# Experts in falling order of their token counts, with 112 to 64 slots by place, in a transformer block kernel on one Trainium2 core

## What is computed

```
def moe_ffn(h, router, w_gu, w_d):
    logits = (h @ router).astype(jnp.float32)
    top_logits, top_idx = lax.top_k(logits, TOP_K)          # TOP_K = 2
    weights = jax.nn.softmax(top_logits, axis=-1)
    combine = jnp.sum(jax.nn.one_hot(top_idx, N_EXPERTS) * weights[..., None], axis=-2)
    for e in range(N_EXPERTS):                              # N_EXPERTS = 8
        out = out + combine[..., e:e + 1] * swiglu(h, w_gu[e], w_d[e])
```

## Time and profile before

| | us |
|---|---|
| median of three runs | 2742.36 |
| span of the profiled execution | 2739.1 |
| expert stage, first gather to end of the last down product | 1580.7 to 2723.0 |
| TensorE busy | 2562.2 (94%) |
| VectorE busy | 654.7 (24%) |
| ScalarE busy | 482.4 (18%) |

### The profile page before, as it was taken

How to read it: one execution, slowest core, us unless ns; L and a number is a source line. 1 busy time by engine, 2 the same in 40 slices (tenths; PEclk the granted TensorE clock), 3 DMA queues, 4 the chain that set the end, 5 groups by cost and what they waited for, 6 DMA issues and landing times.

```text
span 2739.1 us, 61321 instructions
## 1 busy us (share of the span) xinstructions
PE 2562.2 (94%) x28155; PEld 1852.2 (68%) x28156; DVE 654.7 (24%) x1091; ACT 482.4 (18%) x809; POOL 45.5 (2%) x146
## 2 busy tenths in 40 slices
PE   6999878999999998879798899999999999999998
PEld 3564723444478777867786686878778786969593
DVE  1033433000001367737677210000000000000001
ACT  3123013000001265432432310000000000000000
POOL 0000002100000000000000000000000000000000
PEclk9998989999999999989997899999999999999999
DMA  7245004322234600054002278888888888889793
GB/s 250 82 164 184 1 31 154 117 77 77 77 123 159 210 31 3 4 179 169 3 5 73 108 254 324 295 319 306 312 308 317 302 317 302 322 301 336 284 349 138
DMA packets 182197, 504.49 MB, mean 184 GB/s; under 512 B 9586, under 2 KB 73412, under 8 KB 175796
## 3 DMA queue, kind: packets, MB, share of 16 engines
q1 hardware_dynamic: 180148, 494.27, 50.9%
q0 software_dynamic: 1792, 6.19, 0.7%
HBM read 499.38 MB, written 1.05 MB: 183 GB/s over the span
## 4 chain that ended last, share of the span: by engine, by line
PE 55%; DVE 4%; issue 1%; ACT 1%; DMA 0%; POOL 0%; DVEq 0%; ACTq 0%; POOLq 0%
PE banks L1077 25%; PE banks L1094 14%; PE banks L855 7%; PE banks L623 3%; PE banks L1051 1%; PE banks L992 1%; PE banks L1062 1%; PE banks L803 1%; DVE ring_arena L1809 1%; DVE rstd L1915 0%; PE banks L816 0%; DMA ring_arena<-in_rw_a 0%; DVE ring_arena L1814 0%; PE banks L578 0%; DVE rstd L1783 0%
## 5 line engine op out<-in xcount | busy, mean ns | idle before, releaser
L1077 PEld LDWEIGHTS banks<-ring_arena 128*64 128x64 f32 x14336 | 687.1, 137 | 19.1 <-issue 18.2
L1077 PE MATMUL banks<-ring_arena 128*64 128x112 f32 x14336 | 694.0, 259 | 0.0
L1094 PE MATMUL banks<-ring_arena 128*112 128x512 f32 x896 | 385.8, 592 | 0.0
L623 PE MATMUL banks<-ring_arena 128*128 128x256 f32 (+1 forms) x1024 | 314.9, 467 | 15.4 <-DVE ring_arena L1615 9.3
L760 PE MATMUL banks<-ring_arena 128*128 128x512 f32 x704 | 305.4, 597 | 6.4 <-ACT ring_arena L1145 6.1
L1094 PEld LDWEIGHTS banks<-ring_arena 128*112 128x112 f32 x896 | 158.0, 177 | 221.9 <-issue 221.9
L623 PEld LDWEIGHTS banks<-ring_arena 128*128 128x128 f32 x1024 | 195.5, 192 | 134.2 <-issue 102.0
L1998 DVE TENSOR_TENSOR ring_arena<-ring_arena,banks 128x448 f32<-128x448 f32 x32 | 19.9, 621 | 1033.1 <-PE banks L1077 1033.1
L760 PEld LDWEIGHTS banks<-ring_arena 128*128 128x128 f32 x704 | 134.7, 192 | 176.3 <-issue 175.2
L855 PE MATMUL banks<-ring_arena 64*64 64x128 f32 (+1 forms) x6144 | 202.9, 256 | 38.4 <-DVE ring_arena L1814 19.0
L855 PEld LDWEIGHTS banks<-ring_arena 64*64 64x64 f32 x6144 | 190.5, 135 | 45.0 <-issue 32.1
(11 more groups left out here) (304 smaller groups left out, 1831.7 us busy)
## 6 DMA issues: line engine op xcount, KB each, us to landing
ring_arena<-in_moe_w_gu SPq DMA_DIRECT2D x256, 896.0 KB, 5.5
ring_arena<-in_moe_w_d SPq DMA_DIRECT2D x112, 1024.0 KB, 7.0
ring_arena<-in_mod_w SPq DMA_DIRECT2D x48, 1024.0 KB, 6.8
ring_arena<-in_ff_w_gu SPq DMA_DIRECT2D x22, 1024.0 KB, 5.1
ring_arena<-in_ff_w_d SPq DMA_DIRECT2D x22, 1024.0 KB, 4.9
ring_arena<-in_rw_w_rkv SPq DMA_DIRECT2D x20, 1024.0 KB, 5.4
ring_arena<-in_gla_w_in SPq DMA_DIRECT2D x12, 1024.0 KB, 5.6
ring_arena<-in_gla_w_out SPq DMA_DIRECT2D x4, 1024.0 KB, 6.4
```

Of the source, the lines that this page charges most:

```text
L623: ins = T.matmul(b[:, 0:width], w[:, k, j * P:j * P + P], src[:, k, :], start=(k == 0), stop=(k == KT - 1))
L1077: ins = T.matmul(bank[CH * h:CH * h + CH, (c % 4) * CAP:(c % 4) * CAP + CAP], w[:, kk, c * P + CH * h:c * P + CH * h + CH], XG[:, 2 * kp + ...
L1094: ins = T.matmul(ps[6 + h][0:CAP, :], HX[:, 2 * u + k, :], w[:, k, 512 * h:512 * h + 512], start=(u == 0 and k == 0), stop=(u == WD_UNITS ...
```

## The change

Eight slot counts by place, CAPS, take the place of the one CAP. Expert 0 stays first; experts 1 to 7 follow in falling order of their counts, which VectorE sorts (each against each, then sums with a one-hot table). The places are written out on TensorE, ScalarE and VectorE with their slot counts, in place of a loop; SP loads expert 0, waits for `route` and then reads the number of each further expert from a table. TensorE no longer waits for `route`. The masks of expert 0 are made before the sort. Second parts keep CAP slots, and MORE_ITEMS is worked out anew. On ScalarE the copies of the last down product stand before the loop for second parts instead of behind it. GpSimd writes the row of slot counts instead of the table of expert numbers. The storage of the banks keeps its stride of 112. The changed lines, cut to their core:

```diff
-MORE_ITEMS = (2 * SEG - 1) // CAP
+CAPS = (112, 112, 112, 88, 72, 72, 64, 64)
+
+
+def most_overflow():
+
+    most = 0
+    for parts in itertools.product(range(PARTS), repeat=NE):
+        counts, floor = [], 0
+        for e in range(NE - 1, 0, -1):
+            floor = max(floor, CAPS[e] + CAP * (parts[e] - 1) + 1 if parts[e] else 0)
+            counts.append(floor)
+        counts.append(CAPS[0] + CAP * (parts[0] - 1) + 1 if parts[0] else 0)
+        if max(counts) <= SEG and sum(counts) <= 2 * SEG:
+            most = max(most, sum(parts))
+    return most
+
+
+MORE_ITEMS = most_overflow()
+assert all(c + CAP * (PARTS - 1) >= SEG for c in CAPS)
@@ -422,8 +445,10 @@
...
-            with sp.Fori(0, NE) as e:
-                expert(e, e)
+            expert(0, 0)
+            sp.wait_ge(S["route"], 1)
+            with sp.Fori(1, NE) as r:
+                expert(sp.value_load(EXPERT[0:1, bass.ds(r, 1)], min_val=0, max_val=NE - 1), r)
@@ -534,9 +559,9 @@
...
-            pool.wait_ge(S["o_in"], HP)
-            pool.wait_ge(S["b_mm"], HP)
-            g.iota(EXPERT, pattern=[[0, PARTS - 1], [1, NE]], base=0, channel_multiplier=0).then_inc(S["consts"], 1)
+            for e in range(NE):
+                ins = g.memset(CAP_ROW[:, e:e + 1], float(CAPS[e]))
+            ins.then_inc(S["consts"], 1)
@@ -1037,9 +1062,8 @@
...
-            pe.wait_ge(S["route"], 1)
-
-            def scatter(n, q):
+
+            def scatter(n, q, cap):
...
-                T.matmul(ps[4 + h][:, :], PWT[0:CAP, t * P:t * P + P], YS[0:CAP, 512 * h:512 * h + 512],
+                T.matmul(ps[4 + h][:, :], PWT[0:cap, t * P:t * P + P], YS[0:cap, 512 * h:512 * h + 512],
...
-            def item(n, first):
+            def item(n, first, cap=CAP, cap_before=CAP):
@@ -1059,8 +1083,8 @@
...
-                            ins = T.matmul(ps[4 + q][:, (k % 4) * CAP:(k % 4) * CAP + CAP], HTM[:, t, k * P:k * P + P],
-                                           PG[:, t, :], start=(t == 0), stop=(t == 1))
+                            ins = T.matmul(ps[4 + q][:, (k % 4) * CAP:(k % 4) * CAP + cap], HTM[:, t, k * P:k * P + P],
+                                           PG[:, t, 0:cap], start=(t == 0), stop=(t == 1))
@@ -1074,16 +1098,16 @@
...
-                                    ins = T.matmul(bank[CH * h:CH * h + CH, (c % 4) * CAP:(c % 4) * CAP + CAP],
-                                                   w[:, kk, c * P + CH * h:c * P + CH * h + CH], XG[:, 2 * kp + kk, :],
+                                    ins = T.matmul(bank[CH * h:CH * h + CH, (c % 4) * CAP:(c % 4) * CAP + cap],
+                                                   w[:, kk, c * P + CH * h:c * P + CH * h + CH], XG[:, 2 * kp + kk, 0:cap],
...
                     if first:
-                        scatter(n, g)
+                        scatter(n, g, cap_before)
...
-                            ins = T.matmul(ps[6 + h][0:CAP, :], HX[:, 2 * u + k, :], w[:, k, 512 * h:512 * h + 512],
+                            ins = T.matmul(ps[6 + h][0:cap, :], HX[:, 2 * u + k, 0:cap], w[:, k, 512 * h:512 * h + 512],
...
-            with pe.Fori(0, NE) as e:
-                item(e, True)
+            for n in range(NE):
+                item(n, True, CAPS[n], CAPS[max(n - 1, 0)])
             for q in range(4):
-                scatter(NE, q)
+                scatter(NE, q, CAPS[NE - 1])
@@ -1409,27 +1433,34 @@
...
-            def down_out(n):
+            def down_out(n, cap):
                 act.wait_ge(S["wd_used"], WD_RING + WD_UNITS * n)
                 for h in range(2):
-                    C.copy(YS[0:CAP, 512 * h:512 * h + 512], ps[6 + h][0:CAP, :]).then_inc(S["yd_out"], 1)
-
-            def item(n):
-                down_out(n)
+                    C.copy(YS[0:cap, 512 * h:512 * h + 512], ps[6 + h][0:cap, :]).then_inc(S["yd_out"], 1)
...
+            def slots(bank, tiles, cap):
+                return bank[:, 0:tiles * CAP].rearrange("p (a b) -> p a b", a=tiles)[:, :, 0:cap]
+
+            def item(n, cap):
                 for q in range(2):
                     act.wait_ge(S["xg"], 2 * n + q + 1)
...
-                    C.activation(SX[:, 0:4, :], ps[0][:, 0:4 * CAP].rearrange("p (a b) -> p a b", a=4), ACT.Silu).then_inc(S["sil"], 1)
-                    C.activation(SX[:, 4:7, :], ps[1][:, 0:3 * CAP].rearrange("p (a b) -> p a b", a=3), ACT.Silu).then_inc(S["sil"], 1)
+                    C.activation(SX[:, 0:4, 0:cap], slots(ps[0], 4, cap), ACT.Silu).then_inc(S["sil"], 1)
+                    C.activation(SX[:, 4:7, 0:cap], slots(ps[1], 3, cap), ACT.Silu).then_inc(S["sil"], 1)
...
-            with act.Fori(0, NE) as e:
-                item(e)
-            items = second_items(act, lambda x, n: item(n))
-            down_out(items)
+                C.copy(PWT[0:cap, :], ps[4][0:cap, 0:SEG]).then_inc(S["pwt_out"], 1)
+            for n in range(NE):
+                down_out(n, CAPS[max(n - 1, 0)])
+                item(n, CAPS[n])
+            down_out(NE, CAPS[NE - 1])
+
+            def more(x, n):
+                item(n, CAP)
+                down_out(n + 1, CAP)
+            items = second_items(act, more)
@@ -1949,16 +1980,50 @@
...
-            for q in range(PARTS):
-                link(Vv.tensor_tensor(CMB[:, :, NE * q:NE * q + NE], EXL[:, :, :], MX[:, :].unsqueeze(2).to_broadcast([P, 2, NE]), ALU.mult))
+            link(Vv.tensor_tensor(CMB_EXPERT[:, :, :], EXL[:, :, :], MX[:, :].unsqueeze(2).to_broadcast([P, 2, NE]), ALU.mult))
             dve.wait_ge(S["pos"], 1)
 
...
-            for q in range(PARTS):
-                link(Vv.tensor_scalar(RK[:, :, NE * q:NE * q + NE], RK0[:, :, :], -1.0 - float(CAP * q), None, ALU.add))
+            link(Vv.tensor_scalar(RK[:, :, 0:1], RK0[:, :, 0:1], -1.0, None, ALU.add))
+            link(Vv.tensor_copy(COUNTS, ps[5][:, 2 * NE:3 * NE]))
+
+            def slots_of(pos, wt, cap):
+                for t in range(2):
+                    Vv.tensor_scalar(PG[:, t, 0:cap], SLOTS[:, 0:cap], pos[t], None, ALU.is_equal).then_inc(S["pg"], 1)
+                    Vv.tensor_scalar(PW[:, t, 0:cap], SLOTS[:, 0:cap], pos[t], wt[t], ALU.is_equal, ALU.mult).then_inc(S["pg"], 1)
+            slots_of([RK[:, t, 0:1] for t in range(2)], [CMB_EXPERT[:, t, 0:1] for t in range(2)], CAPS[0])
+
...
+
+            def sorted_by_rank(dst, v):
+                link(Vv.tensor_tensor(HOT_TMP, HOT, v, ALU.mult))
+                link(Vv.reduce_sum(dst, HOT_TMP, axis=AX.X))
+            link(Vv.tensor_copy(SORT_KEY, COUNTS))
+            link(Vv.memset(SORT_KEY[:, 0:1], 2.0 * SEG))
+            mine = SORT_KEY.unsqueeze(2).to_broadcast([P, NE, NE])
+            other = SORT_KEY.unsqueeze(1).to_broadcast([P, NE, NE])
+            link(Vv.tensor_tensor(SORT_GT, other, mine, ALU.is_gt))
+            link(Vv.tensor_tensor(SORT_EQ, other, mine, ALU.is_equal))
+            link(Vv.tensor_tensor(SORT_EQ, SORT_EQ, TRI[:, :, :], ALU.mult))
+            link(Vv.tensor_tensor(SORT_GT, SORT_GT, SORT_EQ, ALU.add))
+            link(Vv.reduce_sum(RANK, SORT_GT, axis=AX.X))
+            link(Vv.tensor_tensor(HOT, RANK.unsqueeze(1).to_broadcast([P, NE, NE]), by_rank, ALU.is_equal))
+            sorted_by_rank(ORDER, by_expert)
+            sorted_by_rank(EXCESS, COUNTS.unsqueeze(1).to_broadcast([P, NE, NE]))
+            for t in range(2):
+                sorted_by_rank(RK_SORTED[:, t, :], RK0[:, t, :].unsqueeze(1).to_broadcast([P, NE, NE]))
+                sorted_by_rank(CMB[:, t, 0:NE], CMB_EXPERT[:, t, :].unsqueeze(1).to_broadcast([P, NE, NE]))
+            link(Vv.tensor_scalar(RK[:, :, 0:NE], RK_SORTED[:, :, :], -1.0, None, ALU.add))
+            link(Vv.tensor_tensor(EXCESS, EXCESS, CAP_ROW, ALU.subtract))
+            for t in range(2):
...
             for q in range(PARTS - 1):
-                link(Vv.tensor_scalar(OVER[:, NE * q:NE * q + NE], ps[5][:, 2 * NE:3 * NE], CAP * (q + 1) + 0.5, None, ALU.is_gt))
+                cols = slice(NE * q + NE, NE * q + 2 * NE)
+                link(Vv.tensor_scalar(RK[:, :, cols], RK_SORTED[:, :, :], -1.0 - float(CAP * q), None, ALU.add))
+                link(Vv.tensor_copy(CMB[:, :, cols], CMB[:, :, 0:NE]))
+                link(Vv.tensor_scalar(OVER[:, NE * q:NE * q + NE], EXCESS, CAP * q + 0.5, None, ALU.is_gt))
+                link(Vv.tensor_copy(EXPERT[:, NE * q:NE * q + NE], ORDER))
             link(Vv.memset(BELOW, 1.0))
@@ -1980,30 +2045,34 @@
...
-            with dve.Fori(0, NE) as e:
-                item(e, e, True)
-            items = second_items(dve, lambda x, n: item(x + NE, n, False))
+            for n in range(NE):
+                if n:
+                    gathered(n)
+                    slots_of([RK[:, t, n:n + 1] for t in range(2)], [CMB[:, t, n:n + 1] for t in range(2)], CAPS[n])
+                hidden(n, True, CAPS[n])
+
```

(3 more changed lines are left out.)

36 lines of the change are left out of this document (19 added, 17 removed).

## The result

The changed kernel takes 2692.0 us, the kernel before 2741.1 us beside it on the same chips: ratio 0.9822, 95% interval 0.9809 to 0.9835. It is 49 us faster. The prediction was 139 us faster, 2603.7 us, with a range of 2593 to 2632. The direction held; 88 us of the gain are missing, and the result lies outside the range.

A forecast was written before the change was run, and what follows sets the result against it. TensorE was taken as the bound until loads take over. Start −3.7, places −17.9, −59.8 and −60.2, end +2.9 made −138.7 us; applied to the median of 2742.4 this gave 2603.7 us, eight-in-ten range 2593 to 2632.

The forecast's parts named there:

- What a narrower product costs: Gate/up records on TensorE: 38.3 ns at 88 slots, 31.6 at 72, 29.9 at 64, instead of 48.26.
- When the loads take over: Expert stage: loads at 410 GB/s set a period of 112.4 us at 64 slots; TensorE sets 112.7 at 72, 124.6 at 88.
- The term for the five narrow places: Places 4 to 8: −17.9 us for 88 slots, −59.8 for two of 72, −60.2 for two of 64.
- waits for loads in the last two places: Two places of 64 slots: 112.4 us each by their loads, against 109.6 by TensorE alone.
- a clock that falls in waits: TensorE's granted clock falling in waits for loads of about 0.6 us between units, at two experts' ends; given no case.
- the first rival: Expert weights load at 360 instead of 410 GB/s: four narrow experts about 119.7 us each, 29 us more, 2633; chance 0.15.
- The columns' pace: Gate/up records on TensorE take (2c/2.4 + 3.2)/2 ns for c slots: 38.3 at 88, 31.6 at 72, 28.3 at 64.
- The start: First expert's masks come before the sort, so TensorE's first gather starts 3.7 us earlier.
- The end: ScalarE's second-parts loop now stands behind the last down product's copies, before the first square: 2.9 us later.
- No place spilled: Spill rival: a count over its place's slots in the expert stage adds a ninth pass, 147 us, 2751; chance 0.02.
- The floor rival: Narrow gate records have a higher floor: 2668 us at 40 ns, 2741.6 at 48.26; chance 0.09.
- Its sign for that rival: Records above 32 ns in the last four experts with no wait for loads would prove the forecast record floor wrong.

The follow-up runs named there:

- light_loads: Changed kernel with each gate unit loading only one eighth of its columns, same matmuls, output wrong: 2620.5 us, ratio 0.9565 to the kernel before.
- spread: Changed kernel with each down product cut into three lumps between gate/up groups and ScalarE's last copies behind the second-parts loop: ratio 0.9806 to the kernel before.
- slots112: Changed kernel with 112 slots in every place, all else kept: ratio 0.9995 to the kernel before.
- woven1: As woven, but with down matmuls behind every gate unit instead of every second: 2645.8 us, ratio 0.9672 to the kernel before.
- woven: Changed kernel with down matmuls behind every second gate unit of groups 2 to 4, ScalarE's last copies behind the second-parts loop: 2623.0 us, ratio 0.9596.
- wide1_tail: Changed kernel, narrow places' first column tile per unit one 128-column matmul, not two of 64; ScalarE's last copies behind the second-parts loop: 2675.5 us, ratio 0.9779.

## Why the prediction was wrong

**The step that failed** is the gate time of the narrow places in "What a narrower product costs", and the account of bounds in "When the loads take over". It named three bounds of a record (columns, weight load, loads of weights) and left out the fourth, the supply of instructions. The term for the five narrow places was −137.9 us and measured 662.9 − 5 × 142.54 = −49.8. The 88 us between them come in parts. The gaps are 68.5 us. The records themselves took 70.7 + 124.1 + 119.2 = 314.0 us where 68.6 + 113.3 + 107.2 = 289.1 were forecast, 24.9 more: 34.6 ns a record at 72 slots (124.1 us / 3584) against 31.6 in an uncut group of light_loads. And the 5.6 us that the forecast gave to waits for loads in the last two places (112.4 against 109.6 each) did not come: 68.5 + 24.9 − 5.6 = 87.8.

The 24.9 us have two sources. Each run costs about 0.17 us more than its records alone (4.22 us for 128 at 72 slots, where 128 × 31.6 ns are 4.04), and the chain of the five places has 67 runs: some 11 us. The rest is the clock:

```profile
2416.81 2.70 issue
2419.51 5.50 PE banks L1101 x128
2425.01 0.71 issue
...
2420.00:2422.00 2.00, 2.00 (x44) 2.00 (x42) 0.00 (x0) 0.00 (x0) 0.00 (x0) 0.50 1.03 419
```

Around the end of this gap of 2.70 us the granted clock went from 1.00 to 0.50, the level of 1.2 GHz, and the same 128 records took 5.50 us instead of 3.95. Eight such stretches stand in places 5 to 8, at 1.6 us each (5.50 − 3.95, at 72 slots 5.86 − 4.22) about 13 us by this estimate; behind other gaps of 2.0 to 2.5 us the clock stayed at 1.00. The prediction gave a clock that falls in waits no case. It fell, but here it cost little by itself: the wait behind these 128 records is 0.71 us instead of 2.26, and 5.50 + 0.71 is again 6.21 us. So the stretches at 0.50 are late blocks in another form.

The term was sized from short evidence. That a record of 64 slots takes 29.9 ns came from a run of 192 records in the scan, where DMA is idle; that loads and records do not disturb each other came from rows where records took 48.26 ns, and these leave a block 6.18 us to arrive. Neither row has fast records and full load traffic together, and no row of the trace before has. The sentence in the first rival, that TensorE's instructions come over the same engines and nothing slowed at 421 GB/s, had the right suspect. It drew the wrong inference: nothing slowed because 6.18 us were just enough. One row of the trace before was a warning that I had not read, the waits of TensorE in the scan (us in total, times, longest):

```profile
PE banks L855 <- issue: 12.9, 17, 1.7
```

DMA was idle beside most of them; this window of the kernel before holds 8, 7.9 us in all (columns as above):

```profile
1300.00:1400.00 100.00, 81.86 (x2601) 75.88 (x2604) 67.17 (x118) 39.14 (x59) 0.00 (x0) 0.97 0.01 3
```

The trace gives these waits a size, and I passed over that too. The q8 line of the DMA view between 1357.76 and 1378.19 us, from the end of one such wait to the end of another:

```profile
q8 instruction: 5, 0.08, 1.6%
```

By the trace's record of each packet, four of these start at 1362.41, 1366.35, 1370.48 and 1374.17 us. So with DMA all but idle a block took 3.7 to 4.1 us, against 128 × 29.9 ns = 3.8 us at the forecast pace: the supply stood close to the forecast pace even there. What it becomes beside full traffic, 6.2 us, no row of that trace shows.

The Trainium skill says of this, in "Runtime: NRT & Kernel Launch", section "Instruction fetch mechanics", that instructions are refilled in 16 KiB blocks of 256, and that the cost of crossing a block is "mostly hidden". The block size agrees with the runs of 128 records; the hiding does not, at 2.0 us a block under load. "Advanced Engine Details and Errata", section "ISA Cache", gives lines of 256 instructions and says that there are only two of them. One in use and one ahead would agree with what a lump buys in spread.

**What held.** The columns' pace: 31.6 ns at 72 slots, and 29.5 at 64 in light_loads (13.21 us for 448), as forecast. The wide places at 142.5. The start, −4.0 for −3.7. The end, +3.2 for +2.9, with its cause (the loop ahead of the squares). The sort and the route's delay cost nothing, as slots112 shows. No place spilled: the gate activations ran 32 times, four a place, as before. The rate of loads was no bound, since TensorE never waited for one, so the first rival is out by its cause. The floor rival named 2668 at 40 ns a record and 2741.6 at 48.26; the gate time per record, gaps included, came to 76.8 us / 1792 = 42.9 ns at 72 slots, between the two, but the floor itself was not higher. The measured 2692.0 us lies in the band that the prediction gave the high floor (0.09), by another cause, which is coincidence. Its sign for that rival, records above 32 ns with no wait for loads, misleads too: they took 34.6 and 33.3 ns here, and 31.6 and 29.5 in light_loads.

**What stays open.** Which part of the path delays a block: the size of the loads had no effect, and the depth of the queue could not be tried without starving TensorE. The trace's records of the q8 packets narrow it down. TensorE resumes at 2340.70 us, a packet runs from 2342.65 to 2343.69, TensorE resumes at 2346.91, the next packet runs from 2348.85 to 2349.96, TensorE resumes at 2353.12. So the packet itself takes only 1.0 to 1.1 us of the 6.2; 1.9 us pass before it starts and 3.2 us after it has ended. In the scan, around its wait that ends at 1369.60, the same three parts are 0.9, 1.0 and 2.2 us (packets from 1366.35 to 1367.39 and at 1370.48). Both waiting parts are longer beside the loads, and what happens in them stays open. The scan's waits look like the same bound with its shorter round, but no run changed them.

## What to carry to other kernels

Before making a matmul narrower, count instructions as a resource: 128 fp32 records with their weight loads took up to 6.2 us to arrive under full weight traffic here, and 5.4 to 5.5 us on average, so in the changed kernel the gate records, waits included, did not come under 42 ns (76.0 us / 1792), however few their columns. A cost that nearly equals the present pace is invisible in the profile; look for "issue" in the waits wherever the same engine runs faster elsewhere. When such a bound is met, interleave long instructions with short ones at a grain finer than a block (here 112 to 8), and no finer, as each change of array shape cost 0.12 to 0.17 us.

## What the runs showed of the hardware

- TensorE's instructions come 256 at a time, about one block ahead. A block took up to 6.2 us beside loads at 363 to 394 GB/s (5.4 to 5.5 on average), at most 4.0 us beside 56 GB/s, and 3.7 to 4.1 us in the scan beside 3 GB/s. Its 16 KB packet took 1.0 to 1.1 us of that.
- The granted clock fell from 1.00 to 0.50 behind eight of the waits in places 5 to 8 of the changed kernel and stayed at 1.00 behind the others. In the lines shown the records at the lower clock shortened the next wait (0.71 instead of 2.26 us), so that a block took 6.2 us either way.
- Changing between matmuls on half the array and on all of it cost 0.12 us (192 changes, woven1 against woven; 0.17 us in the wide places alone) and 0.13 us (16 a group, wide1_tail). The Trainium skill, "TensorEngine Tiling (Array Packing)", section "Key Properties", has that changing the tiling mode drains TensorE; the measurements agree that a change costs time, and no run here shows the drain itself.
- Two loads of 896 KB in flight moved 275 GB/s; a deep queue held 384 over 114.5 us.
